# Norms of a two-block network: statistics during the projection, fused scaling, and transposes inside the next stage

## The reference, cut to what matters

```python
x = layer_norm(ALPHA * x + s5_mixer(x), ln_g[0], ln_b[0])
x = layer_norm(ALPHA * x + nsa_mixer(x), ln_g[1], ln_b[1])
h = x
h = h + mix(_rmsnorm(h, attn_norm_g) @ w_in) @ w_out
h = h + _peer(_rmsnorm(h, ffn_norm_g), w_query, sub_keys, u_tab, v_tab)
return _rmsnorm(h, final_norm_g)

def layer_norm(x, g, b):      # mean, var over the 2048 channels
    return (x - mu) * rsqrt(var + LN_EPS) * g + b
def _rmsnorm(x, g):
    return x * rsqrt(mean(x * x) + EPS) * g
```

## Time and profile before

| | us |
|---|---|
| median of three runs | 3267.9 |
| the profiled execution's own time | 3271.05 |
| its span in the trace | 3269.3 |
| PE busy in it | 3063.5 |
| DVE busy | 2158.3 |
| ACT busy | 1490.4 |

### The profile page before, as it was taken

One profiled execution on the slowest core, in us unless ns is written; L12 is line 12 of the kernel. 1 busy time (PEld: TensorE's weight loads), 2 busy tenths in 40 slices (PEclk: granted clock), 3 DMA queues, 4 the chain that ended last, 5 costly groups with the idle time before them and its releaser, 6 DMA issues. The chain is left out here.

```text
span 3269.3 us, 60355 instructions
## 1 busy us (share of the span) xinstructions
PE 3063.5 (94%) x23855; PEld 2516.6 (77%) x23922; DVE 2158.3 (66%) x3046; ACT 1490.4 (46%) x1975; POOL 38.6 (1%) x37
## 2 busy tenths in 40 slices
PE   7796999999986889999979989999999999999997
PEld 6694999988885879998969888776777777777654
DVE  8666544555555775575459999777777777777654
ACT  5433433566642533364344478444444444444443
POOL 1000000000000120000000000000000000000000
PEclk9878999999998899999989999999999999999999
DMA  6224655444443532352645533656555655565554
GB/s 210 70 97 138 226 170 180 154 136 142 137 146 124 155 116 91 117 164 94 206 165 174 172 123 123 199 188 200 192 190 189 202 191 191 187 201 192 187 194 148
DMA packets 143960, 529.90 MB, mean 162 GB/s; under 512 B 16992, under 2 KB 17760, under 8 KB 142048
## 3 DMA queue, kind: packets, MB, share of 16 engines
q1 hardware_dynamic: 140400, 510.33, 48.3%
q10 hardware_dynamic: 3312, 15.92, 1.3%
HBM read 521.99 MB, written 4.19 MB: 161 GB/s over the span
## 5 line engine op out<-in xcount | busy, mean ns | idle before, releaser
L237 DVE TENSOR_TENSOR mem<-mem,rounded 128x1024 bf16<-128x1024 f32 x952 | 1154.2, 1226 | 752.0 <-ACT rounded L231 744.3
L231 ACT CAST rounded<-mem 128x1024 fp32r<-128x1024 f32 x952 | 991.8, 1047 | 1376.5 <-PE ps L264 335.3
L264 PE MATMUL ps<-rounded 128*128 128x256 f32 x3328 | 473.9, 292 | 48.2 <-DVE mem L237 48.2
L264 PEld LDWEIGHTS ps<-rounded 128*128 128x128 f32 x3328 | 422.4, 193 | 53.4 <-issue 26.4
L264 PE MATMUL ps<-mem,rounded 128*128 128x256 bf16 x3328 | 428.8, 276 | 17.9 <-DVE mem L237 17.9
L264 PE MATMUL ps<-rounded,mem 128*128 128x256 bf16 x3328 | 443.8, 279 | 0.0
L264 PEld LDWEIGHTS ps<-mem,rounded 128*128 128x128 bf16 x3328 | 318.6, 99 | 66.0 <-DVE mem L237 17.5
L264 PEld LDWEIGHTS ps<-rounded,mem 128*128 128x128 bf16 x3328 | 315.9, 98 | 61.3 <-issue 1.4
L2489 PE MATMUL ps<-rounded 128*128 128x512 f32 x1024 | 335.7, 441 | 2.1 <-DVE mem L2763 2.1
L2753 DVE TENSOR_TENSOR mem<-mem,ps 128x512 f32<-128x512 f32 x392 | 268.2, 684 | 69.3 <-PE ps L2489 62.7
L2489 PE MATMUL ps<-mem,rounded 128*128 128x512 bf16 x969 | 295.0, 381 | 3.7
(11 more groups left out here) (406 smaller groups left out, 2451.8 us busy)
## 6 DMA issues: line engine op xcount, KB each, us to landing
mem<-experts SPq DMA_DIRECT2D x512, 512.0 KB, 3.7
mem<-weights SPq DMA_DIRECT2D x440, 512.0 KB, 3.6
mem<-x_t SPq DMA_DIRECT2D x4, 512.0 KB, 9.9
mem<-x_rows SPq DMA_DIRECT2D x1, 2048.0 KB, 7.4
mem<-ln_g ACTq DMA_DIRECT2D x2, 1024.0 KB, 4.8
mem<-ln_b ACTq DMA_DIRECT2D x2, 1024.0 KB, 6.9
mem<-cmp_w_k ACTq DMA_DIRECT2D x4, 512.0 KB, 5.5
mem<-cmp_w_v ACTq DMA_DIRECT2D x4, 512.0 KB, 4.5
```

The source lines that it names most:

```text
L231: self.nc.scalar.copy(self.parts(c % SLOTS)[0], self.raw(c % RAW)).then_inc(self.high_done, 1)
L237: self.nc.vector.tensor_tensor(wl, self.raw(c % RAW), wh.bitcast(F32), ALU.subtract).then_inc(self.low_done, 1)
L264: mm = self.nc.tensor.matmul(self.ps[:, bank, half * 256:half * 256 + 256], a, b, start=(part == 0 and n == 0), stop=(part == PIECES - 1 a ...
```

## The change

- `project_residual` is written out tile by tile. It fetches g and b (or g alone) in the midst of its weight stream, on SP's queue, and the statistics are taken while it runs: with the scale of the first block (`ALPHA`) DVE takes `bn_stats` of two times 256 columns behind each tile; with scale 1 ACT squares two times 256 columns with a running sum, two tiles behind.
- `s5_mixer` does the same for the first layer norm: two `bn_stats` of 512 columns behind each of its four last tiles, and the fetches of g and b issued by ACT after each half of the gated values.
- ACT computes an unused root ahead of the block's end in the projections, so that the root's table is loaded.
- A layer norm's scaling is two passes for each row block: (x - mean) x g, and then x 1/root + b. The first pass of row block 0 doesn't wait for the root.
- The separate blocks of the norms and transposes are gone. Norm and transposes stand at the head of `attention`, `second_mixers` and `peer`. PE turns a row block as soon as that one is scaled (`turn_rows`, 16 transposes into four banks). ACT splits the first three pieces ahead of its copies, DVE splits pieces 0 to 2 between the low parts of the turned banks, and PE starts piece n of the first tile once the banks that it reads are split.
- The small loads of a stage, the spill of the rows and the sub-keys are issued by SP at the stage's head, beside the norm.
- In the last step of the expert stage DVE multiplies each finished sum by the final gain, ACT squares it, and after the last one only the statistic and one multiplication are left, shared by DVE and ACT.

```diff
     def project_residual(self, first, n, act, x, scale, dst, upto, stats, loads):
...
             @block.sync
             def _(sp):
+                for i, (to, name, layer) in enumerate(loads):
+                    self.stream(sp, first + 2 + 2 * i, ahead=False)
+                    src = self.ins[name]
+                    sp.dma_start(to, src if layer is None else src[layer]).then_inc(rows_in, 16)
                 self.stream(sp, upto)
...
+                def squares(j):
+                    act.wait_ge(self.bank_free, drained(j))
+                    for tt in range(TT):
+                        a(nc.scalar.activation(stats[:, 64:320], own(j, tt), ACT.Square,
+                                               accum_out=stats[:, n * tt + j:n * tt + j + 1]), squared)
...
+                if scale == 1.0:
+                    squares(n - 2)
+                nc.scalar.activation(self.spare[:, 4:6], self.spare[:, 0:2], ACT.Sqrt)
+                if scale == 1.0:
+                    squares(n - 1)
...
+                        if scale != 1.0:
+                            dve.wait_ge(self.bank_free, drained(j - 1))
+                            for tt in range(TT):
+                                at = 6 * n * tt + 6 * (j - 1)
+                                v(nc.vector.bn_stats(stats[:, at:at + 6], own(j - 1, tt)))
...
+    def norm_centre(self, v, x, g, moments, tt):
+        xs = x[:, tt * D:(tt + 1) * D]
+        v(self.nc.vector.scalar_tensor_tensor(out=xs, in0=xs, scalar=moments[:, 2 * tt:2 * tt + 1], in1=g,
+                                              op0=ALU.subtract, op1=ALU.mult))
+    def norm_scale(self, v, x, out, b, moments, tt, signal):
+        v(self.nc.vector.scalar_tensor_tensor(out=out[:, tt * D:(tt + 1) * D], in0=x[:, tt * D:(tt + 1) * D],
+                                              scalar=moments[:, 8 + tt:9 + tt], in1=b, op0=ALU.mult, op1=ALU.add), signal)
...
@@ attention, scalar @@
+            act.wait_ge(var, 1)
+            nc.scalar.activation(moments[:, 6:8], moments[:, 4:6], ACT.Sqrt).then_inc(root, 1)
+            upto(RAW - HIGH_AHEAD)
+            k.copy_turned(act, hT, h_full, h_high)
...
@@ attention, vector @@
+            k.norm_centre(v, pre, g, moments, 0)
+            dve.wait_ge(root, 1)
+            v(nc.vector.reciprocal(moments[:, 8:10], moments[:, 6:8]))
+            k.norm_scale(v, pre, h1, b, moments, 0, normed)
+            k.norm_centre(v, pre, g, moments, 1)
+            k.norm_scale(v, pre, h1, b, moments, 1, normed)
+            for n in range(8):
+                k.low_turned(dve, hT, n, h_high, h_low)
+                if n >= 3:
+                    upto(min(n - 2, RAW) - LOW_AHEAD)
...
@@ second_mixers, scalar @@
+            for tt in range(TT):
+                act.wait_ge(h2_ready, tt + 1)
+                a(nc.scalar.activation(xn[:, tt * D:(tt + 1) * D], h2[:, tt * D:(tt + 1) * D], ACT.Square,
+                                       accum_out=row_sums[:, tt:tt + 1]), rows_summed)
+                act.wait_ge(msq_ready, tt + 1)
+                nc.scalar.activation(rms_roots[:, tt:tt + 1], msq[:, tt:tt + 1], ACT.Sqrt).then_inc(rms_root, 1)
...
@@ second_mixers, vector @@
+            k.norm_scale(v, pre, h2, b, moments, 0, h2_ready)
+            k.norm_centre(v, pre, g, moments, 1)
+            mean_square(0)
+            k.norm_scale(v, pre, h2, b, moments, 1, h2_ready)
+            scale_rows(0)
+            mean_square(1)
+            scale_rows(1)
...
@@ peer, sync @@
+            sp.dma_start(k.h3_rows, h3).then_inc(k.spilled, 16)
             sp.dma_start(subk, k.ins["sub_keys"]).then_inc(keys_in, 16)
...
@@ peer, vector @@
+                    if j == PAIRS - 1 and part < PIECES - 1:
+                        dve.wait_ge(y_free, 8 * WITH_UP + 2 * part + tt + 1)
+                        v(tt_(final[:, a:a + BANK], y[:, a:a + BANK], f_rows[:, part * BANK:(part + 1) * BANK], ALU.mult),
+                          fin_scaled)
...
+            ts_(final[:, 0:3 * BANK], final[:, 0:3 * BANK], fin[:, 14:15], None, ALU.mult).then_inc(out_first, 1)
+            last_part(0)
+            last_part(1)
```

More of the change, by code:

```diff
@@ L426, in project_residual @@
-    def project_residual(self, first, n, act, x, scale, dst, upto):
-        nc, ps = self.nc, self.ps
-        def rows(a, j):
-            return a.rearrange("p (a n) -> p a n", a=TT)[:, :, bass.ds(j * 256, 256)]
-        with nc.Block() as block:
-            @block.sync
-            def _(sp):
-                self.stream(sp, upto)
+                sp.wait_ge(rows_in, 16 * len(loads))
             @block.tensor
@@ L446, in _ @@
+                if scale == 1.0:
[3 more added lines that the diff above has]
+                    squares(n - 1)
             @block.vector
             def _(dve):
[L448 to L450 removed]
+                v = self.stepper(dve, self.vstep)
@@ L1078, in attention @@
          "turned_copied cmp_copied out_ready out_read z_ready y_ready y_turned y_high").split())
+    pre, h1, moments = k.at(12288, 4096), k.at(H1, 4096), k.at(LN_ST + 48, 16)
+    var, root, normed, h_full, h_high, h_low = (k.sem("ln1_" + n) for n in "var root rows turned high low".split())
     def drained(s):
@@ L1498, in second_mixers @@
     nc, ps = k.nc, k.ps
-    normed_x = k.sem("xn_ready")
     xT = k.split_x(XN_LOW)
-    k.transposes(k.at(8192, 4096), xT, AT_IN2, lambda block: (
-        k.rms_scale(block, k.at(H2, 4096), "attn_norm_g_2", k.at(12288, 2048), k.at(14336, 16), k.at(8192, 4096),
-                    "in2", normed_x) or [(normed_x, TT)]))
+    pre, h2, xn = k.at(18432, 4096), k.at(H2, 4096), k.at(8192, 4096)
+    moments = k.at(LN2_ST + 96, 32)
+    row_sums, msq, rms_roots, rms_rs = (moments[:, 16 + 2 * i:18 + 2 * i] for i in range(4))
+    ln_var, ln_root, h2_ready, rows_summed, msq_ready, rms_root, normed_x, x_full, x_high, x_low = (k.sem("ln2_" + n) for n in (
+        "var root rows sums means rms_root rms_rows turned high low").split())
     first, n_pieces = PIECES * AT_IN2, PIECES * N_IN2
@@ L2305, in peer @@
     hT = k.split_x(HN_LOW)
+    h3, hn, f_st = k.at(H3, 4096), k.at(0, 4096), k.at(FFN_ST, 64)
+    k.h3_rows = nc.dram_tensor("h3_rows", (P, TT * D), F32, kind="Internal").ap()
+    k.spilled, f_mean, f_root, normed, h_full, h_high, h_low = (k.sem("fn_" + n) for n in (
+        "rows_spilled means roots rows turned high low").split())
+    final, f_rows = k.at(0, 4096), k.at(4096, 2048)
+    fin_in, fin_squared, fin_mean, fin_root, fin_recip, fin_scaled, out_first, out_second, out_stored = (
+        k.sem("fin_" + n) for n in "rows squares means roots reciprocals scaled first second stored".split())
+    fin = k.at(6144, 64)
     qry, subk, sc = k.at(QRY, 4096), k.at(SUBK, 2048), k.at(SC, 4096)
@@ L2802, in program @@
     k.new_part()
-    peer_norm(k)
     peer(k)
-    final_norm(k)
 def host_arrays(v):
```

282 lines of the change are left out of this document (154 added, 128 removed).

## The result

Four runs of the changed kernel took 3206.87 to 3217.9 us, median 3213.91; four of the kernel before, beside them, 3265.81 to 3274.27, median 3267.16. The ratio is 0.9824 (95% interval 0.9805 to 0.9844): 53 us faster, where 51.2 were forecast, inside the range and in its likeliest case. The profiled execution took 3213.72 us (span 3211.9). A later set of five runs on another chip gave 3214.57 (experiment 9), beside 3272.06 for sixteen of the kernel before. Two slow runs of that set, one of the kernel before (3931.15 us) and one of prewarm (7044.06 us), are left out of all figures here.

A forecast was written before the change was run, and what follows sets the result against it. PE, busy 94% of the span, bounds the kernel, so time is to be had only where it stands still. Gains 13.3 + 17.5 + 14.7 + 5.7 = 51.2 us take 3267.9 to 3216.7, rounded 3217; range 3206 to 3234.

The forecast's parts named there:

- its likeliest case: Whole kernel: the forecast case, 3207 to 3228 us, given a chance of 0.83.
- the four boundaries: Between stages and at the end, reordered work was to gain 13.3, 17.5, 14.7 and 5.7 us.
- the two squares and the block's change: Third boundary, behind the last sum: ACT's squares put at 1.1 us, block end and `new_part` at 1.56.
- The sub-keys: Third boundary: 1 MB behind the spill's 2 MB, there at 1655.0, a microsecond ahead of PE; late next.
- The wait of a microsecond of DVE for ACT at the second boundary: ACT's three high parts follow the second root, so its first copy ends at 1048.1 and DVE waits a microsecond.
- The fusing: Layer norms: two passes (4.74 us) for three (5.92) bring 1.2 us a row block, not a third.
- The prediction's picture of the first boundary: Most of the 13.3 us gain: statistics 4.6, second turning and splitting 10.2 now against 4.5; fusing little.
- Costs put at nothing: Projections: statistics covered, else 0.8 to 1.5 us a tile; seven 1 MB fetches covered, bounds nothing and 24 us.
- Piece 3's load: Start of a new stage: loading and splitting take 7.6 us against three pieces of 8.2; it just holds.
- The clock at the restart: Stage starts: PE at half clock; between nothing and some 2 us more at each of three boundaries, taken as nothing.
- The table's load: Third boundary and end: two hidden root table loads, 1.28 us each; by the skill's 2.66, sums 2.8 larger.
- The rivals: Fetches paid, 3241 (0.08); no overlap, 3230 (0.04); shift not passed on, 3262 (0.03); fetches delay pieces by whole landings, 3284 (0.02).

The follow-up runs named there:

- experiment 9: The changed kernel run once more, unchanged, on another chip than its first measurement: median 3214.57 us, ratio 0.9832.
- prewarm: The kernel before, plus 78, 40 and 58 idle transposes on PE ahead of its turning at the first three boundaries: median 3272.32 us, ratio 1.0006.
- experiments 11 and 12: Changed kernel, three pieces split ahead of each of first three boundaries and both inner ones, 3209.03 us; the same plus idle transposes at the first three, 3207.2 us.
- experiment 7: Changed kernel with ACT's three high parts moved ahead of its squares at the second boundary: median 3220.49 us, ratio 0.9836.
- experiment 2: Changed kernel with both layer norms in three passes a row block again, the root awaited before the first: median 3223.42 us, ratio 0.9861.
- experiment 1, serial: Changed kernel with the overlap of norm, turning, splitting and products undone at the first three boundaries: median 3233.71 us, ratio 0.9896.
- experiment 5: Changed kernel with the statistics of the first three norms back at the head of the next stage: median 3228.65 us, ratio 0.987.
- experiment 3: Changed kernel with each of seven early 1 MB fetches followed by two more into unused memory, all awaited: median 3223.91 us, ratio 0.9867.
- experiment 6: Changed kernel with the final norm of the kernel before, as its own stage behind the last sum: median 3222.25 us, ratio 0.9846.
- carry: Changed kernel with the next stage's first three pieces already split in the projection's last tile ahead of the first three boundaries: median 3205.16 us, ratio 0.9806.
- carry2warm: Changed kernel, three pieces split ahead of first three boundaries and both inner ones, plus 34, 68 and 30 idle transposes at the first three: 3207.2 us, ratio 0.9801.

## Why the prediction was right

**What bounds the kernel, and the four boundaries.** First 16.67 us against 16.94 forecast (306.4 - 289.46), second 23.93 against 24.1, third 14.20 against 13.6, the end 11.01 against 11.0. The method carried: the order of work on each engine written out anew, with durations from rows. The step with the largest miss is the third boundary: the two squares and the block's change were put at 2.66 and took 3.08 (1610.36 - 1607.28). The squares were right, 1.08 against 1.1 (they end at 1608.36); the change of block took 2.00, not 1.56. The stretch from there to the product ran 0.2 longer. The sub-keys, named as what is late next, did not come late: PE's wait of 0.80 us there names DVE, and they landed 9.3 us after their issue at 1610.70, 1.5 us ahead of the product. With the boundary shortened further they did (experiments 11 and 12: 0.53 and 1.96 us). The wait of a microsecond of DVE for ACT at the second boundary was 0.76, and experiment 7 took 0.73 of it back.

**The fusing.** 1.2 us a row block, forecast and measured (experiment 2: 1.23), with 0.45 more a norm for the root off the path.

**Where the gain comes from.** Undone one at a time: statistics 10.9, overlap 12.3, fusing 5.8, end 5.8, early fetches 18.4. They add up to 53.2 where the change brought 51.1, but that sum is luck. The fetch and the statistics overlap each other at the head (before, DVE waited only 0.35 us for b behind them at the first boundary), so each undone alone counts some of the same microseconds twice; no run undid both. And what is left, such as one boundary in place of two ahead of the mixers, was not undone. The prediction's picture of the first boundary, 4.6 for statistics and the rest of most of it from the second turning and splitting, holds for the statistics (4.4); for the overlap experiment 1 shows 4.7 there, not the 5.7 (10.2 - 4.5) that I read out of the two stretches; why it is a microsecond less was not looked into.

**Costs put at nothing.** The statistics in the projections cost nothing that shows (experiment 5). The seven fetches cost nothing: the changed kernel's PE has no new wait in either projection, and experiment 3 shows how near the limit is. Piece 3's load just held: after the first boundary no wait of PE for DVE's low parts stands between 308.66 and the output projection.

**The clock at the restart** is the one term that was wrong. I took nothing, "as a short idle time was enough to show 0.50 there", with 0 to 2 us a boundary as its bound. The three starts gained 1.6, 2.0 and 2.1 us in the profiled run; in experiment 9 only the third did. These 5.7 us are most of the 8.8 that the three stages behind the boundaries gained; the first stage lost 2.5, which nothing had forecast either. The median's gain, 53.3 against 51.2, may have it from there, but 2 us are within the scatter of four runs (3206.87 to 3217.9), so that it came so near is in part luck.

**The table's load.** With the old end (experiment 6) the load took 1.28 us and the root followed 0.02 us behind it. The end gained 5.8, near the 5.7 that the row's figure gives. By the rule of the Trainium skill ("ScalarE: Activation LUTs", What ACT_TABLE_LOAD costs) it would have been 1.4 more; no drain shows in this trace.

**The rivals.** The forecast case came; none of the rivals did. The shift was passed on whole at every boundary, and the stages behind them did not grow.

## What to carry to other kernels

Where the busiest engine stands still only at boundaries, write out the boundary's order on each engine and add up the rows; this gave the stretches to within 0.6 us. Take statistics where their inputs come into being, and move their constants' loads with them: here the load at its old place would have cost 18.4 of the 51 us. A fused pass is worth what its row says, 1.2 us for a block, not its share of the count of passes.

## What the runs showed of the hardware

**The start of a stage.** In 42 starts (three in each of 14 profiled executions) the mean granted clock of the stretch was 0.99 to 1.00 (2.4 GHz) in 25, 0.70 to 0.84 (in part at 1.2 GHz) in 16 and 0.93 in one. Between the kernel before and the changed one the difference was 1.6 to 2.1 us each. The third boundary's start was at full rate in the 11 executions in which PE stood 0 to 2.0 us at the first product, and slow in the three with 3.4 us or more (before, serial, prewarm). The second sorts likewise, full with up to 2.7 us and slow with 3.0 or more, but the changed kernel and experiment 9, one program, stand on either side of it (2.30 and 3.01). The first doesn't sort: with 0.57 us of standing it was 0.99 in the changed kernel and 0.81 in experiment 9, and 1.00 in serial with 3.12. So what decides it stays open.

**The first stage's clock moves the whole time.** Up to its last sum the kernel took 282.81 to 292.72 us over these executions, with no edit that explains it. The stretch of 175 to 200 us in the changed kernel and in carry:

```profile
175.00:200.00 25.00, 25.00 (x228) 24.81 (x224) 20.99 (x25) 3.19 (x2) 0.00 (x0) 0.50 0.01 1
```

```profile
175.00:200.00 25.00, 25.00 (x336) 24.79 (x335) 24.05 (x29) 2.11 (x3) 0.00 (x0) 0.61 0.01 1
```

PE is busy throughout, at 1.2 GHz (0.50) in the first and part of the time at 2.4 in the second, with 228 and 336 matmuls. The kernel before made 230 there, at 0.50. The whole first stage differs by 9.2 us between those two; the attention with its projection spans 707.0 to 710.3 us over the executions in which no edit lies inside it, the mixers with theirs 567.7 to 572.4. This is why edits of a few microseconds were judged by their own stretch.

**Transposes and the clock.** 78 transposes of the identity in a row took 8.71 us, 0.112 each, at a granted clock of 1.00. The 16 of a row block took 3.68 us, 0.23 each, at 0.50 in the changed kernel (both halves of the first boundary) and 1.97, 0.123 each, at 1.00 in carry2warm (the first half of its first turning). So the factor of two is the clock. Transposes alone also brought the clock up: in prewarm, 40 of them behind 21.94 us of idle time began at 0.50 and ran at a mean of 0.91 in their last 2.7 us.
